# A fused two-block layer on one core: the last side product moved ahead of the keys, two norms applied to finished banks, and the first output input written earlier

## The reference, cut to what matters

```python
# first block, mamba2 mixer: 4 groups of 512 features, each with its own norm, then the output product
yg = y.reshape(b, s, 4, 512)
yg = yg * rsqrt(mean(yg * yg, axis=-1) + EPS)
x = x + gate * ((yg.reshape(b, s, 2048) * norm_g) @ out_w)
# then keys and values from the normed x
hk = modulate(x, kv_norm_g, kv_shift, kv_scale)          # rmsnorm(x) * (1 + scale) + shift
kv = hk @ kv_w
# second block, its last line: a gate product and a side product of an input p (512 x 256)
h3 = rmsnorm(x, norm_ple_g)
x = x + sigmoid(h3 @ w_ple_gate) * (p @ w_ple_proj)
```

## Time and profile before

| | us |
|---|---|
| median of 3 runs | 1604.35 |
| lowest, highest | 1603.04, 1608.87 |
| the profiled execution's own time | 1607.12 |
| its span, first to last instruction | 1605.3 |
| PE busy | 1554.6 (97% of the span) |
| DVE busy | 942.1 (59%) |
| ACT busy | 680.3 (42%) |
| POOL busy | 112.3 (7%) |

### The profile page before, as it was taken

One profiled execution on the slowest core, in us unless ns is written; L12 is line 12 of the kernel. 1 busy time (PEld: TensorE's weight loads), 2 busy tenths in 40 slices (PEclk: granted clock), 3 DMA queues, 4 the chain that ended last, 5 costly groups with the idle time before them and its releaser, 6 DMA issues. The chain is left out here.

```text
span 1605.3 us, 19593 instructions
## 1 busy us (share of the span) xinstructions
PE 1554.6 (97%) x7998; PEld 1234.2 (77%) x7998; DVE 942.1 (59%) x1171; ACT 680.3 (42%) x959; POOL 112.3 (7%) x77
## 2 busy tenths in 40 slices
PE   6999999999899999999999999999999999999998
PEld 3788877767689766677888786678888888888877
DVE  3769799896673666754367536654553444433253
ACT  4555676654432555653222355533432222222241
POOL 0000000124200000022000000000110000000120
PEclk8999999999999999999999999999999999999999
DMA  7434334323582211123121122122222322332333
GB/s 318 159 131 162 143 125 141 138 82 141 199 325 81 78 53 34 46 80 108 57 76 53 53 80 92 66 79 82 102 79 105 106 82 101 105 111 82 109 144 118
DMA packets 47385, 177.76 MB, mean 111 GB/s; under 512 B 3616, under 2 KB 20256, under 8 KB 31680
## 3 DMA queue, kind: packets, MB, share of 16 engines
q1 hardware_dynamic: 30368, 167.44, 28.4%
q10 hardware_dynamic: 16928, 9.06, 2.2%
HBM read 172.23 MB, written 4.26 MB: 110 GB/s over the span
## 5 line engine op out<-in xcount | busy, mean ns | idle before, releaser
L642 PE MATMUL bank<-HH,whi 128*128 128x512 f32 x1352 | 555.6, 411 | 10.3 <-DVE HL L1101 5.7
L644 PE MATMUL bank<-HH,wlo 128*128 128x512 f32 x1352 | 529.6, 392 | 0.0
L643 PE MATMUL bank<-HL,whi 128*128 128x512 f32 x1352 | 529.2, 391 | 0.0
L1147 DVE TENSOR_TENSOR wlo<-raw,whi 128x2048 fp32r<-128x2048 f32 (+2 forms) x118 | 267.3, 2265 | 117.8 <-ACT whi L1824 116.4
L642 PEld LDWEIGHTS bank<-HH,whi 128*128 128x128 f32 x1352 | 255.2, 189 | 91.7 <-issue 44.6
L644 PEld LDWEIGHTS bank<-HH,wlo 128*128 128x128 f32 x1352 | 254.9, 189 | 54.8
L643 PEld LDWEIGHTS bank<-HL,whi 128*128 128x128 f32 x1352 | 255.6, 189 | 48.0 <-issue 3.1
L1824 ACT ACTIVATE whi<-raw 128x2048 fp32r<-128x2048 f32 (+2 forms) x118 | 222.3, 1884 | 113.8 <-PE bank L644 113.7
L2382 POOL TENSOR_TENSOR SR<-SR,tmp 128x512 f32<-128x512 f32 x30 | 55.2, 1842 | 578.3 <-ACT tmp L1844 577.4
L672 PE MATMUL bank<-whi,HH 128*128 128x256 f32 x256 | 74.3, 290 | 0.0
L673 PE MATMUL bank<-whi,HL 128*128 128x256 f32 x256 | 72.4, 283 | 0.0
(11 more groups left out here) (310 smaller groups left out, 2127.7 us busy)
## 6 DMA issues: line engine op xcount, KB each, us to landing
raw<-wstream SPq DMA_DIRECT2D x113, 1024.0 KB, 4.8
aslot<-tstream SPq DMA_DIRECT2D x24, 512.0 KB, 3.3
A<-astream SPq DMA_DIRECT2D x8, 1024.0 KB, 18.1
AC<-scratch ACTq DMA_DIRECT2D x16, 512.0 KB, 5.4
QT<-tstream SPq DMA_DIRECT2D x12, 512.0 KB, 5.1
OZ<-tstream SPq DMA_DIRECT2D x12, 512.0 KB, 7.7
raw<-wstream SPq DMA_DIRECT2D x4, 768.0 KB, 4.3
X<-xT SPq DMA_DIRECT2D x1, 2048.0 KB, 8.1
```

What stands on the lines that cost most here:

```text
L642: e.matmul(o, wh[:, k, c], hi[:, kb0 + k, :], start=first and k == 0, stop=False)
L643: e.matmul(o, wh[:, k, c], lo[:, kb0 + k, :], start=False, stop=False)
L644: x = e.matmul(o, wl[:, k, c], hi[:, kb0 + k, :], start=False, stop=last and k == kb - 1)
L1147: e.tensor_tensor(wlo[:, i % 2, 0:n], raw[:, i % 2, 0:n], whi[:, i % 2, 0:n].bitcast(F32), ALU.subtract).then_inc(s_lo, 1)
```

## The change

Four edits:

1. The chunk of `w_ple_proj_2` moves in the plan from behind `fd` to between the output product and the keys. PE does its 48 matmuls behind out 31, with the two matmuls of the norm's sum in the middle (after two of the eight outputs). p is loaded into `PR` in the middle of the output product and split into tiles of its own (`PH`, `PL`); ACT's eight copies (to `PO`) stand in its queue ahead of the eight HH of the keys; the writes to `pscr` stand in SP's queue ahead of the third key chunk's load.
2. At the end the gate product takes X times the gain, without the norm's factor: ACT and DVE write HH and HL while `fd` runs, PE starts pg 0 and pg 1 k by k, does the sum after three k, and DVE multiplies each finished bank by the factor R; the sigmoid (ACT) reads that product. `last_out(n)`, the multiplication by PP and the addition to X, stands in DVE's queue behind the product with R of block n + 1.
3. Group 3 of the output product likewise: HH and HL come from Y times the gain, DVE makes HL instead of POOL, and DVE multiplies each of the banks out 24 to 31 by R (into a tile of Y) before it adds it to X. Four multiplications of Y are gone.
4. `out_split(0)` on ACT stands ahead of the reading of z 15, and waits for single k steps of z 15 (`s_hk2`) instead of its end.

```diff
@@ weight_plan
             plan.append((_cols("m_out_w", 512 * i, 512, 4 * g, 4), [("out", 8 * g + 4 * i + j) for j in range(4)]))
+    plan.append((_cols("w_ple_proj_2", 0, 1024, 0, 2), [("pp", n) for n in range(8)]))
...
-    plan.append((_cols("w_ple_proj_2", 0, 1024, 0, 2), [("pp", n) for n in range(8)]))
@@ SP
+        w.wait_ge(s_y, 16)
+        e.dma_start(PR[:, :, :], pT).then_inc(l_x, 16)
         weave((chain(out_proj(2), out_proj(3)), 66), (ada_blocks(20, 24, 1, 24), 16))
+        behind("pp", 0)
...
+        for n in range(8):
+            w.wait_ge(s_pp, n + 1)
+            e.dma_start(pscr[n], PO[n % 3][:, :]).then_inc(l_pw[n % 3], 16)
@@ PE, blocks and the stretch behind out 31
+                    elif b == ("z", 15) and k < 4:
+                        x.then_inc(s_hk2, 1)
...
-        sum_of("out", aux[0], T[0][:, :])
+        for n in range(8):
+            if n == 2:
+                sum_of("out", aux[0], T[0][:, :])
+            o, c = aux[1 + n % 4][:, :], slice(128 * n, 128 * n + 128)
...
+            w.wait_ge(s_pp, n - 3)
+            for k in range(2):
+                h_ready("p")(k)
+                e.matmul(o, wh[:, k, c], PH[:, k, :], start=(k == 0), stop=False)
...
@@ PE, end (the side product's loop is removed here)
+        first = both("pg", 0, "ple")
+        run(take(first, 3))
+        sum_of("fd", aux[0], T[0][:, :])
+        run(first)
+        for n in range(2, 8):
             run(block("pg", n, "ple"))
@@ DVE
+            elif kind == "out" and idx > 23:
+                w.wait_ge(s_rr, SUM_AT["y3"])
+                own(e.tensor_tensor(Y[:, idx % 8, :], bank_of(kind, idx)[:, :], R, ALU.mult))
+                x = e.scalar_tensor_tensor(X[:, k, :], Y[:, idx % 8, :], ada[:, gate + k:gate + k + 1], X[:, k, :],
+                                           ALU.mult, ALU.add)
...
+        for n in range(8):
+            if n % 2 == 0 and n > 0:
+                behind("pg", n)
+            w.wait_ge(s_blk, blk_done("pg", n))
+            e.tensor_tensor(T[n % 3][:, :], bank_of("pg", n)[:, :], R, ALU.mult).then_inc(s_pgr, 1)
+            if n > 0:
+                last_out(n - 1)
+        last_out(7)
@@ ACT
+                if hb == 39:
+                    out_split(0)
...
+        behind("pp", 0)
         lnexp()
-        w.wait_ge(s_sum, SUM_AT["out"])
-        rsqrt(aux[0][:, :], D, R[:, :]).then_inc(s_rr, 1)
+        for n in range(8):
+            if n == 2:
+                w.wait_ge(s_sum, SUM_AT["out"])
+                w.wait_ge(s_res, 32)
+                rsqrt(aux[0][:, :], D, R[:, :]).then_inc(s_rr, 1)
+            w.wait_ge(s_ppm, n + 1)
+            w.wait_ge(l_pw[n % 3], 16 * (n // 3))
+            e.activation(PO[n % 3][:, :], aux[1 + n % 4][:, :], ACT.Copy).then_inc(s_pp, 1)
         for k in range(8):
             high_shifted("kv", k, ada[:, 24:32])
```

More of the change, by code:

```diff
@@ L260, in program @@
     OZ = sbt("OZ", [128, NB, S], F32, ph)
+    ph3 = ExitStack()
+    PR = sbt("PR", [128, 2, S], F32, ph3)
+    PH, PL = (sbt(n, [128, 2, S], F32R, ph3) for n in ("PH", "PL"))
+    PO = [sbt(f"PO{i}", [128, S], F32, ph3) for i in range(3)]
+    ph3.close()
     W = sbt("W", [128, 14, S], F32, ph)
@@ L593, in _ @@
                 chunk(chunk_of["fd", 2 * i4] + c)
-        behind("pp", 0)
-        for n in range(8):
-            w.wait_ge(s_pp, n + 1)
-            e.dma_start(pscr[n], pstage[n % 3][:, :]).then_inc(l_pw[n % 3], 16)
         for i4 in range(4):
@@ L801, in _ @@
         w.wait_ge(s_xd, 16)
-        sum_of("out", aux[0], T[0][:, :])
+        w.wait_ge(s_rr, SUM_AT["y3"])
+        w.wait_ge(s_y, 16)
+        w.wait_ge(s_st, 12)
+        i = chunk_of["pp", 0]
+        wh, wl = (t[:, i % 2, :].rearrange("p (k n) -> p k n", k=2) for t in (whi, wlo))
+        for n in range(8):
+            if n == 2:
+                sum_of("out", aux[0], T[0][:, :])
+            o, c = aux[1 + n % 4][:, :], slice(128 * n, 128 * n + 128)
+            w.wait_ge(s_hi, i + 1)
+            w.wait_ge(s_lo, i + 1)
+            w.wait_ge(s_pp, n - 3)
+            for k in range(2):
+                h_ready("p")(k)
+                e.matmul(o, wh[:, k, c], PH[:, k, :], start=(k == 0), stop=False)
+                e.matmul(o, wh[:, k, c], PL[:, k, :], start=False, stop=False)
+                x = e.matmul(o, wl[:, k, c], PH[:, k, :], start=False, stop=(k == 1))
+            x.then_inc(s_ppm, 1)
         def feature(kind, n, stage):
@@ L1320, in ssd @@
                 yield
[L1321 removed]
+                if 0 < g < 4 and c == 2:
                     w.wait_ge(s_rr, SUM_AT[f"y{g - 1}"])
@@ L1369, in out_proj @@
                 residual("out", 8 * g + n, n, 16)
+                if g == 2 and n == 3:
+                    o = VOFF["m_norm_g"][0] + 12
+                    for q in range(4):
+                        low_gained("out3", 4 + q, Y[:, 12 + q, :], cv[:, o + q:o + q + 1])
+                if g == 3 and n == 0:
+                    w.wait_ge(l_x, 32)
+                    for k in range(2):
+                        low("p", k, PR[:, k, :])
                 yield
@@ L1772, in _ @@
             f_low(2 * i11)
-        rest(chunk_of["fd", 0] - 1)
-        for k in (6, 7):
-            w.wait_ge(l_x, 48)
-            low("p", k, T[k - 5][:, :])
+        pg = vcol("ple_g")
         for n in range(8):
-            if n % 2 == 0 and n > 0:
+            if n % 2 == 0:
                 rest(chunk_of["fd", n] - 1)
-            if n % 2 == 0:
                 rest(chunk_of["fd", n])
@@ L1917, in tanh, with out_split @@
                 e.activation(t_of[hb, "h"][:, :], bank_of(kind, idx)[:, :], ACT.Tanh, scale=0.5).then_inc(s_th, 1)
+        def out_split(g):
+            for q in range(4):
+                if g == 3:
+                    w.wait_ge(s_y, 16)
+                else:
+                    w.wait_ge(s_yn, 4 * g + q + 1)
+                if g == 0:
+                    w.wait_ge(s_hk2, q + 1)
+                else:
+                    w.wait_ge(s_blk, blk_done(*(("z", 15) if g == 1 else ("out", 8 * g - 9))))
+                if g == 3:
+                    o = VOFF["m_norm_g"][0] + 12 + q
+                    e.activation(HH[:, 4 + q, :], Y[:, 12 + q, :], ACT.Copy, scale=cv[:, o:o + 1]).then_inc(s_hh, 1)
+                else:
+                    high_of(Y[:, 4 * g + q, :], 4 * (g % 2) + q)
         def in_proj(g):
@@ L1998, in _ @@
             weave((in_proj(g), 80), (take(chunks, 16), 16))
-        def out_split(g):
-            for q in range(4):
-                w.wait_ge(s_yn, 4 * g + q + 1)
-                w.wait_ge(s_blk, blk_done(*(("z", 15) if g < 2 else ("out", 8 * g - 9))))
-                high_of(Y[:, 4 * g + q, :], 4 * (g % 2) + q)
         def out_proj(g):
@@ L2017, in out_proj @@
                     out_split(g + 1)
-        out_split(0)
+                if n == 5 and g == 2:
+                    w.wait_ge(l_x, 32)
+                    for k in range(2):
+                        e.activation(PH[:, k, :], PR[:, k, :], ACT.Copy).then_inc(s_hh, 1)
         weave((chain(out_proj(0), out_proj(1)), 66), (chunks, 28))
         run(chain(out_proj(2), out_proj(3)))
+        behind("pp", 0)
         lnexp()
-        w.wait_ge(s_sum, SUM_AT["out"])
-        rsqrt(aux[0][:, :], D, R[:, :]).then_inc(s_rr, 1)
+        for n in range(8):
[6 more added lines that the diff above has]
+            e.activation(PO[n % 3][:, :], aux[1 + n % 4][:, :], ACT.Copy).then_inc(s_pp, 1)
         for k in range(8):
@@ L2115, in _ @@
         next(proj)
+        for n in range(3):
+            w.wait_ge(l_pw[n], (48, 48, 32)[n])
         weave((attention(), 111), (proj, 120))
@@ L2460, in _ @@
             add_x("fd", 2 * i4 + 1)
-        for k in range(1, 8, 2):
-            low("ple", k, T[k % 3][:, :])
     ctx.close()
```

98 lines of the change are left out of this document (28 added, 70 removed).

## The result

The changed kernel takes **1611.51 us** (median of 20 runs, 1605.09 to 1614.93). The kernel before was run 20 times beside it, the three at first among them: median 1608.42 (1603.04 to 1610.09). The ratio is 1.0023 with a 95% interval of 1.0012 to 1.0033: 0.23% slower, and the interval lies wholly above 1. The prediction said 1600.6, range 1596.0 to 1605.5. Both its sign and its range were wrong.

What follows compares the result with a forecast made beforehand. PE, busy 97% of the span, was taken as the bound. Terms -12.3 + 1.8 + 8.2 - 1.6, with 0.2 for POOL's adds, gave -3.7 us: from the median 1604.35 to 1600.6 us, range 1596.0 to 1605.5.

Steps and rivals of the forecast that it cites:

- (c): Out 31 to the keys: side product fills PE's idle time, copies cost at most 0.1 us, 2.3 us idle before keys.
- W: Experiments' theory, not the forecast's: side product copies wait for writes standing behind 4 MB of loads; 6.0 us measured.
- (d): Second key chunk: its split, queued behind all eight HH, makes PE wait 2.7 us; second pair starts 8.2 us later.
- (e): Out 0: its split moves under z 15, gaining 1.6 us, because the wait for XW grows.
- (f): Group 3 of the output product: DVE's changed work makes no bank late; 0, up to +1 us.
- (a): End, PE: 48 side matmuls (10.9 us) and 1.4 us of waits go; -12.3 us.
- (b): End, tail behind PE's last matmul: more DVE passes and later PP loads; +1.8 us.
- S: Rival: the 2.3 us wait before the keys drops the clock through the first pair; 1607.5 us, chance 0.06.
- F: Rival: second key chunk's split does not bind and out 0 gives its full 3.1 us; 1596.2 us, chance 0.14.
- N: Rival: DVE falls behind in the gate product and PE stops four times, 1 us each; 1604.6 us, chance 0.05.
- T: Rival: a drain with ACT's table load makes the first copy late, 1.3 us more; 1601.9 us, chance 0.05.

Runs made afterwards that it cites:

- run 20: Not a label but a count: the kernel before was run 20 times beside the changed kernel; median 1608.42 us.
- po8: The changed kernel with eight PO tiles instead of three, so no copy waits for a write; median 1604.44 us, 0.9986 of the kernel before.
- wfirst: The changed kernel with SP issuing the eight pscr writes ahead of the eight tstream loads; median 1603.69 us, 0.9976 of the kernel before.
- split: po8 with ACT's split of the second key chunk placed between its sixth and seventh HH of the keys; 1603.90 us, 0.9967 of the kernel before.
- nog3po8: The changed kernel with edit 3 undone and eight PO tiles instead of three; median 1599.99 us, 0.9950 of the kernel before.
- nog3: The changed kernel with edit 3 undone, three PO tiles kept; median 1608.24 us, 1.0006 of the kernel before.
- e12: The changed kernel with edits 3 and 4 undone, so edits 1 and 2 alone; median 1610.57 us, 1.0012 of the kernel before.
- mix: po8 with ACT writing the keys' HH n - 3 behind copy n instead of all eight behind the last copy; 1600.75 us, 0.9953 of the kernel before.
- tail: mix with DVE finishing each gate block right behind its product with R; median 1598.84 us, 0.9940 of the kernel before.

## Why the prediction was wrong, point by point

- **(c), the stretch before the keys: the step that failed.** It counted PE's wait for the copies and said "no more than 0.1 us of wait". It left out ACT's own wait: copy n needs the write of copy n - 3 to have landed. And it counted the write's effect on SP only forwards (the third key chunk behind it), not what stands ahead of it, eight loads of 512 KB. The order on ACT was right up to the third copy: the first copy was put at 434.4, less the 1.8 us that all is earlier 432.6, and starts at 433.08. Then come 6.00 us of ACT's idle time and 4.42 us of PE's, and the clock falls to 1.2 GHz. Cost, by `po8` and `wfirst`: 6.0 us of the 6.6 that this stretch is over its prediction. With W taken away (c) holds: 2.17 us before the keys against 2.3, and 29.7 us against 29.1 to the second pair.
- **(d), the second chunk: right**, as `po8` (2.42 us) and `split` show. The fixed distance held: in the changed kernel the chunk's rest ends 13.65 us behind the first HL's end, for 13.67 before. Only 0.62 us of the wait is left there, since the first pair ran partly at half clock, as before: it was a cost behind another.
- **(e), out 0: right in size (-1.8 for -1.6), by luck.** I had the wait for XW grow from 1.44 to about 3 us, and overlooked the one of 1.54 us at 339.40 behind it. The two become one of 1.93, so the sum of group 3 is 3.45 us earlier, the first dip already paid. Then the second dip takes 1.7 of that back. Two errors cancel.
- **(f), group 3: 0 was wrong.** I asked whether a bank is read late, and none is. What counts is when the last X is there, and two instructions for each residual make DVE's last stretch longer, so that square, sum and copies are later. Part of this was in (c), which had the last X at 430.5 (less 1.8: 428.7; it is there at 429.3) and gave the side product 13.2 us; it takes 12.7 in `nog3po8` and 13.8 in `po8`, so the edit costs 1.1 us with eight tiles, and about half of that had been counted. With three tiles the traces of `nog3` and the change differ by 1.5 us. The whole times say more, 3.3 and 4.5 us by the medians, 2.7 and 5.8 by the ratios; that size is open.
- **(a), the end: right**, -12.5 for -12.3. **(b), the tail: right within its error**, +1.3 for +1.8. DVE waited once for PP, 2.22 us at 1584.16 for block 2, and none of it reached the end.
- **The base.** Three runs gave 1604.35; 20 give 1608.42. I carried the 2.8 us between the profiled execution and that median over to the forecast, which made it 1600.6 and not 1603.4. So of the 10.9 us by which the median missed, 4.1 lie in the base and 6.8 in the sum.
- **The rivals.** S (clock) came true in part: the clock fell, but behind the wait of 4.42 us that S did not know, not behind the 2.3. In `nog3po8` it did fall behind that wait (2.17 us), and as the prediction said of a clock that stays above 0.75 over the pair (about 0.87 here), the second wait covered most of it (2.42 became 0.85). F did not: the second chunk binds wherever the clock is up. N did not: no wait between the blocks of the gate product. T did not: the first copy starts 0.01 us behind the table load's end (433.08 against 431.79 + 1.28). The Trainium skill (ScalarE: Activation LUTs, "What ACT_TABLE_LOAD costs") would have a drain of some 1.38 us there; neither this trace nor the earlier trace rows has one.

What stays open: what makes one wait of about 2 us draw a dip and another not; and why edit 3's cost is larger in the whole times than in the traces.

## What to carry to other kernels

When work is moved to another place, follow its results to memory as well: a buffer that is reused waits for the landing of its write, and here a write of 256 KB behind 4 MB of loads landed only when these were nearly through. Issue the small transfer first, or give it a buffer of its own. And price an added instruction on an engine with slack by the last result of the stage, not by whether a buffer is read in time.

## What the runs showed of the hardware

- A write of 256 KB landed 2.0 us after its issue where it stood ahead of the 4 MB of loads in SP's queue (`wfirst`), and 8.1 us after it where it stood behind them (the change).
- Waits of PE of about 2 us (1.78 to 2.82) were followed by some 3.5 us at 1.2 GHz in some places and executions and not in others. Before, the waits of 1.79 us at 317.05 and 2.62 us in the earlier trace rows's stretch at 784 to 796 had none; in `e12` the first of them (PE, windows) had one:

```profile
317.44 0.47 PE L644 MATMUL bank<-HH,whi 128*128 128x512 f32 x1 [1.78 <-POOL HL L2405]
```

```profile
318.00:322.00 4.00, 3.64 (x13) 2.66 (x12) 3.97 (x4) 3.97 (x10) 3.16 (x3) 0.64 0.00 0
```

- A profile's mean clock goes with its time: for the kernel before 0.994 with about 1603 us and 0.989 with about 1608.5; for the changed one 0.992 with 1605.5 and 0.984 with 1614.4. A dip is 1.7 us, and the start alone can be 4.6 us apart (`po8` and `mix`); which of the two makes this spread isn't shown, since each kernel was traced once (the one of `tail` twice). Three runs do not give this kernel's median to half a microsecond: here they were 4 us off.
